# Layer norms with the variance by token on partitions, and one modulation sum moved into the routing

## The chip, the cores and the metric

One core of one Trainium2 chip. The metric is the device time of one launch in microseconds (us): the median of several runs. All five engines of the core are used: TensorE (PE), VectorE (DVE), ScalarE (ACT), GpSimd (POOL) and SyncE (SP), which issues the DMAs.

## What is computed

One inference step of a trunk of four layers on 384 tokens (128 of context, 256 latent) with a width of 1024. The mixer of layer i is gMLP, SSD, HGRN2 and gMLP again; behind each stands a mixture of 16 experts. Each half of a layer ends in a layer norm, so there are eight:

```python
def layer_norm(x, g, b):
    mu = jnp.mean(xf, -1, keepdims=True)
    var = jnp.mean(jnp.square(xf - mu), -1, keepdims=True)
    return (xf - mu) * lax.rsqrt(var + LN_EPS) * g + b

sh1, sc1, g1, sh2, sc2, g2 = modulation(cond, w_mod[li], b_mod[li])
h = x * (1 + sc1) + sh1
x = layer_norm(ALPHA * x + g1 * mixer(h), ln_g[li, 0], ln_b[li, 0])
h = x * (1 + sc2) + sh2
x = layer_norm(ALPHA * x + g2 * moe(h), ln_g[li, 1], ln_b[li, 1])
```

`modulation` is silu(cond) @ w_mod + b_mod, 1024 x 6144 for each layer. The SSD mixer has an RMS norm of its own ahead of its output matrix.

## The kernel before

Activations lie with features on partitions: `x`, `y` and `h32` are 8 tiles (KD) of 128 features by 384 tokens (T), and NT = 3 blocks of 128 tokens. Every engine runs its own hand-written order; semaphores order them, and `claim(bank, ...)` makes TensorE wait until a PSUM bank's last reader is through. Dense products of the mixers split both operands in a high and a low part (ACT makes `whi`, POOL `wlo`) and take three products.

The norm of `q` (0 to 7; two for each layer, 2l behind the mixer and 2l+1 behind the experts): `mean_step` adds each residual tile as it comes, with a 128x128 matrix of 1/D as weights, so that bank 6 holds the mean of each token on all partitions. DVE subtracts it in four pieces (L1765), ACT squares them (L1275), `variance(q)` multiplies the same matrix with the 8 square tiles into bank 5 (L1508, 384 columns), ACT takes the root of 128x384 (L1277), DVE the reciprocal of 128x384 (L1768), and then eight times multiplies a tile (L1770) and modulates it (L1755). ACT and, behind the experts, POOL make `x`, `hh` and `hl` of each tile. In layer 1 `squares(j)` (L718) does the same for the RMS norm, beside the SSD's last steps, and root and reciprocal follow (L575, L853); the result scales each out tile (L857).

The out stage (`out_tiles`) makes 8 tiles with `full`; DVE adds each to the residual, and the mean step of a tile follows one tile later. Modulation is worked out beside it: w_mod comes in chunks of 1 MB, 24 for each layer in 6 groups of 4. DVE multiplies a chunk into `macc` (`mod_chunk`, L1722 and L1725, four operations), and when a group is through TensorE sums over partitions (`mod_sum`, L1492: 16 products, which the trace shows as 32 instructions, with `macc` as weights and one column of ones) and DVE takes the result (`mod_take`, L1733). `out_mods` says which chunks lie ahead of which out tile, for SP's loads and for DVE, and `sums_after` after which tile the sum stands: after tile 3 and tile 7 in layers 0 and 1, after tile 7 in layers 2 and 3. The sum after tile 7 of layers 0 to 2 is the next layer's first group (6l+6); that of layer 3 is its own last group.

All loads go through SP's one queue in the order of `stream_plan`. In the mixers they rotate through four narrow slots of 1 MB (RAW = 4): a load waits until the chunk four places earlier is used up, an out chunk by TensorE, a mod chunk by DVE. The experts use eight slots.

Behind norm 2l stands the routing: router products of 16 columns (L1586), transposes (L1577), group ranks (L1597, L1599), then DVE works out slots and the `spread` matrices (L1881), and TensorE gathers the tokens (L1609, L1610) ahead of the experts (L1646, L1661).

## Time and profile before

| | us |
|---|---|
| median of 3 runs | 3042.9 (3038.44 to 3047.69) |
| the profiled execution | 3040.79, of which its span is 3039.0 |
| TensorE busy | 2660.4 (88%) |
| DVE busy | 1495.8 (49%) |
| POOL busy | 800.3 (26%) |
| ACT busy | 745.4 (25%) |
| mean granted clock of TensorE | 0.916 |

The profile is of one execution. Line numbers are those of the kernel before. A timeline row gives the start and the length of one or more instructions of a line in us, and in brackets how long the engine was idle ahead and what ended that. TensorE's instructions are pipelined, so a row's length holds the drain of its last one; the distance from one start to the next is its price in a stream. PEclk is the granted clock, as a share of 2.4 GHz.

### The profile page before, as it was taken

The numbers are of one execution on the slowest core, as the hardware profiler recorded it, in microseconds if no ns is written. First come the engines' busy times: TensorE is split into PE (matmuls) and PEld (weight loads), VectorE is DVE, ScalarE is ACT, GpSimd is POOL, SyncE is SP. The second block draws the span as 40 slices with busy tenths as digits, with TensorE's granted clock in tenths as the row PEclk, the third lists the DMA queues.
The fourth block names the chain that finished last, engine by engine and source line by source line (L and its number), as shares of the span: only waits on it lengthen the run. The fifth ranks groups of instructions, "written<-read, shape, count | busy, mean of one in ns | idle before, by whom it ended". The sixth has DMA issues, their size and how long they took to land.

```text
span 3039.0 us, 30686 instructions
## 1 busy us (share of the span) xinstructions
PE 2660.4 (88%) x11926; PEld 1949.3 (64%) x11926; DVE 1495.8 (49%) x2416; ACT 745.4 (25%) x1253; POOL 800.3 (26%) x501
## 2 busy tenths in 40 slices
PE   1679889998897888899998877778999989989997
PEld 1679864445896778744457866667444589974444
DVE  7445543333649876533334478875333326650012
ACT  0123130001453342310014243333100144231001
POOL 1346400001453344000014457650000146600000
PEclk9889879999799999799998887788999999979999
DMA  6543638893231215388943410113889433437881
GB/s 222 166 125 98 185 108 326 320 363 125 87 120 33 66 59 163 115 299 323 352 173 117 139 59 18 33 58 124 299 323 351 174 111 111 125 125 256 298 302 50
DMA packets 291855, 524.44 MB, mean 173 GB/s; under 512 B 9472, under 2 KB 141056, under 8 KB 291328
## 3 DMA queue, kind: packets, MB, share of 16 engines
q1 hardware_dynamic: 288256, 519.33, 49.3%
q10 hardware_dynamic: 3456, 3.15, 0.3%
q8 instruction: 96, 1.57, 0.2%
q14 instruction: 47, 0.39, 0.0%
HBM read 517.73 MB, written 4.72 MB: 172 GB/s over the span
## 4 chain that ended last, share of the span: by engine, by line
PE 74%; DVE 14%; issue 4%; ACT 4%; DMA 3%; POOL 2%; ACTq 0%; SPq 0%; DVEq 0%
PE ps L1646 22%; PE ps L1661 11%; PE ps L1458 6%; PE ps L1459 6%; PE ps L1460 6%; PE ps L1492 3%; DVE macc L1725 3%; PE ps L1508 2%; PE ps L1481 2%; PE ps L1482 2%; PE ps L1483 2%; POOL wlo L1391 1%; DVE h L1755 1%; PE ps L654 1%; PE ps L1500 1%
## 5 line engine op out<-in xcount | busy, mean ns | idle before, releaser
L1391 POOL TENSOR_TENSOR wlo<-ring,whi 128x1024 fp32r<-128x1024 f32 x202 | 525.5, 2616 | 1515.2 <-ACT whi L1263 1515.2
L1646 PE MATMUL ps<-ring,xg 128*128 128x512 f32 x1536 | 705.3, 604 | 0.0
L1646 PEld LDWEIGHTS ps<-ring,xg 128*128 128x128 f32 x1536 | 289.5, 194 | 327.9 <-issue 327.5
L1725 DVE SCALAR_TENSOR_TENSOR macc<-ring,cond_s,macc 128x1024 f32<-128x1024 f32 x336 | 452.8, 1409 | 0.0
L1936 DVE SCALAR_TENSOR_TENSOR hid<-ps,cws,sg 128x256 f32<-128x256 f32 x96 | 46.4, 483 | 671.4 <-ACT sg L1356 671.4
L1661 PE MATMUL ps<-ring,hidt 128*128 128x512 f32 x768 | 351.7, 601 | 2.3 <-ACT hidt L1330 2.3
L1458 PE MATMUL ps<-hh,whi 128*128 128x384 f32 x832 | 306.2, 368 | 28.3 <-POOL wlo L1391 18.4
L1263 ACT ACTIVATE whi<-ring 128x1024 fp32r<-128x1024 f32 x202 | 206.9, 1054 | 352.7 <-DMA ring<-gmlp_w_out 115.8
L1459 PE MATMUL ps<-hl,whi 128*128 128x384 f32 x832 | 291.0, 350 | 0.0
L1460 PE MATMUL ps<-hh,wlo 128*128 128x384 f32 x832 | 290.8, 350 | 0.0
L1661 PEld LDWEIGHTS ps<-ring,hidt 128*128 128x128 f32 x768 | 147.9, 193 | 188.7 <-issue 188.7
L1330 ACT ACTIVATE hidt<-ps 128x256 f32<-128x256 f32 x96 | 36.9, 384 | 750.8 <-PE ps L1636 750.8
L1481 PE MATMUL ps<-whi,hh 128*128 128x256 f32 x480 | 144.8, 302 | 67.3 <-POOL wlo L1391 58.8
L1458 PEld LDWEIGHTS ps<-hh,whi 128*128 128x128 f32 x832 | 167.0, 201 | 37.6 <-POOL wlo L1391 20.0
L1459 PEld LDWEIGHTS ps<-hl,whi 128*128 128x128 f32 x832 | 166.9, 201 | 0.7 <-issue 0.5
L1460 PEld LDWEIGHTS ps<-hh,wlo 128*128 128x128 f32 x832 | 165.9, 199 | 0.0
L1481 PEld LDWEIGHTS ps<-whi,hh 128*128 128x128 f32 x480 | 99.6, 207 | 69.8 <-POOL wlo L1391 59.7
L1482 PE MATMUL ps<-whi,hl 128*128 128x256 f32 x480 | 142.9, 298 | 0.0
L1483 PE MATMUL ps<-wlo,hh 128*128 128x256 f32 x480 | 142.5, 297 | 0.0
L1492 PE MATMUL ps<-ones,macc 128*128 128x1 f32 x768 | 100.2, 264 | 46.2 <-DVE macc L1725 46.2
L1492 PEld LDWEIGHTS ps<-ones,macc 128*128 128x128 f32 x768 | 101.8, 215 | 52.3 <-issue 31.5
L1458 PE MATMUL ps<-gsh,whi 128*128 128x384 f32 x256 | 91.0, 355 | 19.8 <-POOL wlo L1391 19.2
(325 smaller groups left out, 4175.3 us busy)
## 6 DMA issues: line engine op xcount, KB each, us to landing
ring<-moe_w_gu SPq DMA_DIRECT2D x192, 1024.0 KB, 7.5
ring<-w_mod SPq DMA_DIRECT2D x96, 1024.0 KB, 7.6
ring<-moe_w_down SPq DMA_DIRECT2D x96, 1024.0 KB, 5.3
ring<-gmlp_w_in SPq DMA_DIRECT2D x32, 1024.0 KB, 5.7
ring<-ssd_w_in SPq DMA_DIRECT2D x21, 1024.0 KB, 5.3
ring<-hgrn_w_in SPq DMA_DIRECT2D x20, 1024.0 KB, 5.2
ring<-gmlp_w_out SPq DMA_DIRECT2D x16, 1024.0 KB, 5.8
ring<-ssd_w_out SPq DMA_DIRECT2D x8, 1024.0 KB, 5.9
```

Source lines behind the costliest of these rows:

```text
L1263: act.activation(split_sub(whi, s0), raw_sub(s0), ACT.Copy).then_inc(S["hi_ready"], 1)
L1391: pool.tensor_tensor(split_sub(wlo, s0), raw_sub(s0), split_sub(whi, s0).bitcast(F32), ALU.subtract).then_inc(S["lo_ready"], 1)
L1458: pe.matmul(out, lhi, rhi, start=first, stop=False)
L1459: pe.matmul(out, lhi, rlo, start=False, stop=False)
L1460: return pe.matmul(out, llo, rhi, start=False, stop=last)
L1481: pe.matmul(outs[t], hh[:, k, tk], pair(whi, k), start=(k == 0), stop=False)
L1482: pe.matmul(outs[t], hl[:, k, tk], pair(whi, k), start=False, stop=False)
L1483: ins = pe.matmul(outs[t], hh[:, k, tk], pair(wlo, k), start=False, stop=(k == KD - 1))
L1492: ins = pe.matmul(ps[:, 7, 2 * j + v:2 * j + v + 1], macc[:, v, j * P:(j + 1) * P], ones[:, 0:1], start=True, stop=True)
L1646: ins = pe.matmul(ps[:, s % 2, :], xg[:, w, k, :], whole(what, s, 4)[:, k % 4, :], start=(k == 0), stop=(k == KD - 1))
L1661: ins = pe.matmul(ps[:, OUT_BANKS[w % 2][h], :], hidt[:, s % 2, k, :], whole("D", s, 2)[:, k, 512 * h:512 * h + 512], start=(e == 0 and k ...
L1725: ins = dve.scalar_tensor_tensor(out=macc[:, v, :], in0=w[:, k, :], scalar=by, in1=macc[:, v, :], op0=ALU.mult, op1=ALU.add)
```

## The change

Variance: the squares become the weights and one column of the 1/D matrix moves, one product for each of 8 tiles and 3 token blocks, so that the variance of a token lies on its partition, in 3 columns of bank 7. Root and reciprocal work on 128x3. TensorE spreads the result: for each block it multiplies the column, broadcast to 128x128, with the identity, which puts it for each token on all partitions of bank 7, where DVE's multiplication reads it. The RMS norm of layer 1 is made the same way, but with a copy by ACT to SBUF; TensorE waits for the reciprocal ahead of its out products, and DVE's reciprocal stands ahead of `start_residual`.

The next layer's first modulation sum (group 6l+6) leaves the end of the out stage; TensorE does it behind the ranks, and DVE takes it behind the route. `out_mods` gives every tile one chunk until there are none, which changes layer 3 alone (tiles 0 to 3 in place of 1, 3, 5, 7), and its sum stands after tile 3.

```diff
--- before.py
+++ after.py
@@ -147,7 +147,8 @@
 
     todo = ([(l, MODC - MOD_GROUP + j) for j in range(MOD_GROUP)] if l % 3 < 2 else []) + \
            ([(l + 1, j) for j in range(MOD_GROUP)] if l + 1 < DEPTH else [])
-    return todo[c * len(todo) // outs:(c + 1) * len(todo) // outs]
+    each = max(1, len(todo) // outs)
+    return todo[c * each:(c + 1) * each]
 
 
 class Chain:
@@ -230,8 +231,8 @@
 
         sq = ar("ln_sq", [P, KD, T], F32, 0)
         h32 = ar("h32", [P, KD, T], F32, 12)
-        std = ar("ln_std", [P, T], F32, 84)
-        rstd = ar("ln_rstd", [P, T], F32, 86)
+        std = ar("ln_std", [P, NT], F32, 84)
+        rstd = ar("ln_rstd", [P, NT], F32, 86)
 
         macc = ar("macc", [P, 2, D], F32, 76)
 
@@ -295,6 +296,7 @@
         sgy = ar("sgy", [P, 2, T], F32, 81)
         ssq = ar("ssq", [P, 2, T], F32, 84)
         srr = ar("srr", [P, T], F32, 87)
+        rms = ar("rms", [P, 2, NT], F32, 88.5)
         sout = ar("sout", [P, 2, T], F32, 0)
         s0 = yr("s0", [P, 2, 512], F32, 0)
         s1 = yr("s1", [P, 2, 512], F32, 4)
...
@@ -572,7 +574,9 @@
                     act.activation(syh[:, j - 1, :], sgy[:, (j - 1) % 2, :], ACT.Copy).then_inc(S["syh_ready"], 1)
             feed(sb((l, "out")) + 3)
             act.wait_ge(S["rms_done"], 16)
-            act.activation(srr[:, :], bank(6), ACT.Sqrt, bias=eps[:, 0:1], scale=0.5).then_inc(S["rms_std"], 1)
+            act.activation(rms[:, 0, :], ps[:, 6, T:T + NT], ACT.Sqrt, bias=eps[:, 0:1], scale=0.5).then_inc(S["rms_std"], 1)
+            act.wait_ge(S["rms_spread"], 1)
+            act.activation(srr[:, :], bank(6), ACT.Copy).then_inc(S["srr_ready"], 1)
             for m in range(8):
                 feed(sb((l, "out"), 2 * m + 2) + 3)
 
@@ -715,10 +719,12 @@
 
             def squares(j):
                 pe.wait_ge(S["gsq_ready"], j + 1)
-                pe.matmul(bank(6), mean_d[:, :], ssq[:, j % 2, :], start=(j == 0),
-                          stop=(j == 15)).then_inc(S["rms_done"], 1)
-
-            claim(6, "rms_std", 1)
+                for t in range(NT):
+                    ins = pe.matmul(ps[:, 6, T + t:T + t + 1], ssq[:, j % 2, toks(t)], mean_d[:, 0:1], start=(j + t == 0),
+                                    stop=(j == 15 and t == NT - 1))
+                ins.then_inc(S["rms_done"], 1)
+
+            claim(6, "srr_ready", 1)
             for j in range(16):
                 if j % 2 == 0 and j < 8:
                     f = SCAN_Z + j // 2
@@ -730,6 +736,10 @@
                     squares(j - 2)
             squares(14)
             squares(15)
+            pe.wait_ge(S["rms_rec"], 1)
+            for t in range(NT):
+                ins = pe.matmul(ps[:, 6, toks(t)], rms[:, 1, t:t + 1].to_broadcast([P, P]), ident[:, :], start=True, stop=True)
+            ins.then_inc(S["rms_spread"], 1)
             out_tiles(l, syh, syl, 2, "syl_ready", 0)
 
         def dve_ssd(dve, l, link, start_residual, residual, out_chunk_mods, mod_take):
@@ -847,10 +857,11 @@
                 if j >= 2:
                     dve.wait_ge(S["syl_ready"], j - 1)
                 dve.tensor_scalar(sgy[:, j % 2, :], xs[:, j, :], c_("sng", j), None, ALU.mult).then_inc(S["gy_ready"], 1)
+            dve.wait_ge(S["rms_std"], 1)
+            dve.reciprocal(rms[:, 1, :], rms[:, 0, :]).then_inc(S["rms_rec"], 1)
             start_residual(2 * l)
             dve.wait_ge(S["syl_ready"], 16)
-            dve.wait_ge(S["rms_std"], 1)
-            link(dve.reciprocal(srr[:, :], srr[:, :]))
+            dve.wait_ge(S["srr_ready"], 1)
             for m in range(KD):
                 out_chunk_mods(l, m, 1)
                 dve.wait_ge(S["sub_done"], nth[sb((l, "out"), 2 * m + 1)] + 1)
@@ -1245,11 +1256,7 @@
 
         def sums_after(l, m):
 
-            if l % 3 == 2:
-                done = {7: 6 * l + 6}
-            else:
-                done = {3: 6 * l + 5, 7: 6 * l + 6} if l + 1 < DEPTH else {7: 6 * l + 5}
-            return [done[m]] if m in done else []
+            return [6 * l + 5] if l % 3 < 2 and m == 3 else []
 
         @block.scalar
         def _(act):
@@ -1274,7 +1281,7 @@
                     act.wait_ge(S["diff_ready"], 4 * q + j + 1)
                     act.activation(sq[:, 2 * j:2 * j + 2, :], y[:, 2 * j:2 * j + 2, :], ACT.Square).then_inc(S["sq_ready"], 1)
                 act.wait_ge(S["var_done"], q + 1)
-                act.activation(std[:, :], bank(5), ACT.Sqrt, bias=eps[:, 0:1]).then_inc(S["std_ready"], 1)
+                act.activation(std[:, :], ps[:, 7, T:T + NT], ACT.Sqrt, bias=eps[:, 0:1]).then_inc(S["std_ready"], 1)
                 l, w = q // 2, q % 2
                 for k in range(KD):
                     act.wait_ge(S["norm_ready"], 8 * q + k + 1)
@@ -1502,11 +1509,17 @@
                     ins.then_inc(S["mean_done"], 1)
 
             def variance(q):
-                claim(5, "std_ready", q + 1)
+                claim(7, "norm_ready", 8 * q + 8)
                 for k in range(KD):
                     pe.wait_ge(S["sq_ready"], 4 * q + k // 2 + 1)
-                    ins = pe.matmul(bank(5), mean_d[:, :], sq[:, k, :], start=(k == 0), stop=(k == KD - 1))
+                    for t in range(NT):
+                        ins = pe.matmul(ps[:, 7, T + t:T + t + 1], sq[:, k, toks(t)], mean_d[:, 0:1], start=(k + t == 0),
+                                        stop=(k == KD - 1 and t == NT - 1))
                 ins.then_inc(S["var_done"], 1)
+                pe.wait_ge(S["rstd_ready"], q + 1)
+                for t in range(NT):
+                    ins = pe.matmul(ps[:, 7, toks(t)], rstd[:, t:t + 1].to_broadcast([P, P]), ident[:, :], start=True, stop=True)
+                ins.then_inc(S["rstd_spread"], 1)
 
             def out_tiles(l, rhi, rlo, halves, ready, count):
 
@@ -1598,6 +1611,8 @@
                 for u in range(NT):
                     ins = pe.matmul(ps[:, 4, 12:16], ones_b[:, :], gone[:, u, :], start=(u == 0), stop=(u == NT - 1))
                 ins.then_inc(S["rank_done"], 1)
+                if l + 1 < DEPTH:
+                    mod_sum(6 * l + 6)
 
                 pe.wait_ge(S["tlo_ready"], 2 * NT * (l + 1))
                 pe.wait_ge(S["spread_ready"], NT * (l + 1))
@@ -1765,9 +1780,10 @@
                     dve.tensor_tensor(y[:, 2 * j:2 * j + 2, :], y[:, 2 * j:2 * j + 2, :],
                                       bank(6).unsqueeze(1).to_broadcast([P, 2, T]), ALU.subtract).then_inc(S["diff_ready"], 1)
                 dve.wait_ge(S["std_ready"], q + 1)
-                link(dve.reciprocal(rstd[:, :], std[:, :]))
+                dve.reciprocal(rstd[:, :], std[:, :]).then_inc(S["rstd_ready"], 1)
+                dve.wait_ge(S["rstd_spread"], q + 1)
                 for k in range(KD):
-                    dve.tensor_tensor(y[:, k, :], y[:, k, :], rstd[:, :], ALU.mult).then_inc(S["norm_ready"], 1)
+                    dve.tensor_tensor(y[:, k, :], y[:, k, :], bank(7), ALU.mult).then_inc(S["norm_ready"], 1)
                     if not last:
                         dve.wait_ge(S["norm_ready"], 8 * q + k + 1)
                         modulate(y, k)
@@ -1915,6 +1931,8 @@
                 for i in range(NT):
                     tokens_low(l, i)
                 route(l)
+                if l + 1 < DEPTH:
+                    mod_take(6 * l + 6)
                 dve.wait_ge(S["cws_done"], l + 1)
                 dve.tensor_reduce(cws[:, :, :], ps[:, 5, 0:2 * EG * NW].rearrange("p (w h e) -> p w e h", h=2, e=EG), AX.X,
                                   ALU.add).then_inc(S["cws_ready"], 1)
```

## Rows read from the trace of the kernel before

**Rows 1.** The page's chain of work that ended last, by engine.
```profile
PE 74%; DVE 14%; issue 4%; ACT 4%; DMA 3%; POOL 2%; ACTq 0%; SPq 0%; DVEq 0%
```
**Rows 2.** Timeline, layer 0's first norm: start us, us, engine, line, operation [idle before].
```profile
385.33 3.63 PE L1492 MATMUL ps<-ones,macc 128*128 128x1 f32 x32
388.82 2.25 PE L1500 MATMUL ps<-y_t,mean_d 128*128 128x384 f32 x4
393.15 6.97 PE L1508 MATMUL ps<-ln_sq,mean_d 128*128 128x384 f32 x16 [2.08 <-ACT ln_sq L1275]
...
400.77 2.55 DVE L1768 RECIPROCAL ln_rstd<-ln_std 128x384 f32<-128x384 f32 x1 [6.05 <-ACT ln_std L1277]
403.36 0.56 DVE L1770 TENSOR_TENSOR y_t<-y_t,ln_rstd 128x384 f32<-128x384 f32 x1
```
**Rows 3.** Groups by form, variance products: count | busy us, mean ns | idle before.
```profile
L1508 PE MATMUL ps<-ln_sq,mean_d 128*128 128x384 f32 x128 | 55.2, 596 | 16.6 <-ACT ln_sq L1275 16.6
```
**Rows 4.** Timeline, TensorE, the first modulation sum of the kernel.
```profile
25.78 6.96 PE L1492 MATMUL ps<-ones,macc 128*128 128x1 f32 x32 [25.78 <-DVE macc L1725]
```
**Rows 5.** Timeline, TensorE: sum and first variance product, layers 1, 2 and 3.
```profile
1230.42 4.84 PE L1492 MATMUL ps<-ones,macc 128*128 128x1 f32 x32
...
1240.11 0.98 PE L1508 MATMUL ps<-ln_sq,mean_d 128*128 128x384 f32 x1 [2.08 <-ACT ln_sq L1275]
...
2069.14 3.96 PE L1492 MATMUL ps<-ones,macc 128*128 128x1 f32 x32
...
2077.95 0.98 PE L1508 MATMUL ps<-ln_sq,mean_d 128*128 128x384 f32 x1 [2.08 <-ACT ln_sq L1275]
...
2678.87 3.63 PE L1492 MATMUL ps<-ones,macc 128*128 128x1 f32 x32
...
2686.49 0.98 PE L1508 MATMUL ps<-ln_sq,mean_d 128*128 128x384 f32 x1 [2.08 <-ACT ln_sq L1275]
```
**Rows 6.** Windows: us, busy (count) by engine, then PEclk, DMA share, GB/s.
```profile
1233.00:1240.00 7.00, 5.03 (x15) 3.27 (x15) 2.65 (x8) 0.86 (x2) 0.00 (x0) 0.50 1.00 368
2679.00:2683.00 4.00, 4.00 (x35) 3.83 (x34) 1.17 (x5) 0.00 (x0) 0.77 (x1) 1.00 0.93 356
420.20:423.50 3.30, 0.26 (x10) 0.17 (x7) 2.99 (x13) 0.60 (x1) 0.00 (x0) 1.00 0.00 0
1269.00:1273.00 4.00, 0.00 (x0) 0.00 (x0) 3.66 (x15) 0.32 (x1) 0.00 (x0) 0.50 0.00 0
```
**Rows 7.** Timeline, TensorE, layer 0's second norm: last product, first variance product.
```profile
745.50 0.34 PE L1683 MATMUL ps<-back,olo 128*128 128x384 f32 x1
...
749.67 0.56 PE L1508 MATMUL ps<-ln_sq,mean_d 128*128 128x384 f32 x1 [2.08 <-ACT ln_sq L1275]
```
**Rows 8.** Timeline lines for the small operations, and the SSD residual's group.
```profile
2015.22 0.28 ACT L935 ACTIVATE hrt<-ps,eps 128x24 f32<-128x24 f32 x1
...
430.49 0.18 DVE L1901 RECIPROCAL rt<-rt 128x3 f32<-128x3 f32 x1
...
2000.17 1.65 PE L1070 MATMUL ps<-uw 128*128 128x128 f32 x6
...
L857 DVE TENSOR_TENSOR sout<-ps,srr 128x384 f32<-128x384 f32 x8 | 4.4, 556 | 22.7 <-PE ps L1460 22.7
```
**Rows 9.** Timeline, TensorE, layer 0's routing: the first gather product.
```profile
425.47 0.76 PE L1609 MATMUL ps<-spread,thi 128*128 128x512 f32 x1 [5.01 <-DVE spread L1881]
```
**Rows 10.** Timeline, TensorE, out stages: layer 0's tiles 0 and 2, layer 3's tile 0.
```profile
290.79 0.42 PE L1458 MATMUL ps<-gsh,whi 128*128 128x384 f32 x1
...
322.38 0.66 PE L1458 MATMUL ps<-gsh,whi 128*128 128x384 f32 x1 [11.34 <-POOL wlo L1391]
...
2601.22 0.42 PE L1458 MATMUL ps<-gsh,whi 128*128 128x384 f32 x1
```
**Rows 11.** Timeline, layer 1's out stage: ACT's root, TensorE's tile 2.
```profile
1150.33 0.58 ACT L575 ACTIVATE srr<-ps,eps 128x384 f32<-128x384 f32 x1
...
1170.65 0.66 PE L1458 MATMUL ps<-syh,whi 128*128 128x384 f32 x1 [6.86 <-POOL wlo L1391]
```

## What the change will do to the time

> **What bounds the kernel now.** I read the chain of work that ended last first: TensorE carries 74% of it, DVE 14% [rows 1]. So I walk TensorE's timeline through each stage that the diff touches and ask what it waits for there. Around each of the eight layer norms all work is in one line: mean, differences, squares, variance product, root, reciprocal, first multiplication [rows 2]. A microsecond won or lost there is one of the whole. TensorE's time depends on its granted clock, 1.00 (2.4 GHz) or 0.50 (1.2 GHz), so I read that for each stretch too.
>
> **The norm itself, before.** In layer 0 the variance takes 6.97 us (16 instructions: each fp32 product is two). From its end (400.12) to the first multiplication (403.36) it is 3.24 us, of which the reciprocal is 2.55 [rows 2]. All eight variances together are busy for 55.2 us [rows 3]: 6.9 each. Layer 0's 0.44 us an instruction lies between 0.32 and 0.64, which is 768 columns (384 in two passes) at 2.4 and at 1.2 GHz: 5.1 or 10.2 us for 16.
>
> **Variance after.** 8 x 3 products of one column with the squares as weights, in two passes: 48 instructions. The nearest rows are the modulation sums, 32 instructions of exactly that form (128x128 fp32 weights, one column): 3.49 us from the first to the next line's start at the high clock [rows 2], 6.96 us at the low one [rows 4]. That is 0.109 and 0.218 us each, so 48 take 5.2 or 10.45 us. At either clock this equals the 384-column form: fewer columns win nothing, since the weights' load is the price. What differs is the clock. Sums of one column let it fall: in layer 1 the sum began at 1230.42 at full clock and the clock was 0.50 by 1233.00; in layer 3 it began at 2678.87 and was still at 1.00 at 2683.00 [rows 5, 6]. So it falls between some 2 and a little over 4 us after wide products stop. The new variance starts 2.08 us after the mean's last product [rows 7], under that same kind of work, and wants 5.2 us: in all eight norms the clock falls inside it, after 0 to 3.4 us, and nothing in it brings it back (today's wide variance does). I take 1.7 us at full clock: 2 x 5.2 - 1.7 = 8.8 us (rounded up), 70.4 for eight. Against 55.2 that is **+15.2 us** (all of it low: +28.4; all high: -13.6).
>
> The Trainium skill ("TensorE: Matmul & The Clock Gate", LDWEIGHTS) prices a weight load by its columns alone, 128/1.2 = 107 ns, without the clock. It matches the high-clock row and not the low-clock row (218 ns), so the measurement decides. By the page an estimate for 48 would be 5.1 us always, and the sum would be some 29 us less; its time is in rival A.
>
> **Root, reciprocal and spread after.** The root of 24 columns took 0.28 us, the reciprocal of 3 columns 0.18 [rows 8]; I take 0.25 for 3 columns from the first. The spread is 6 instructions of 128 columns. Six of that form took 1.65 us at the low clock [rows 8], which is where the variance leaves it. With five hand-overs of about 0.04 us: 0.25 + 0.18 + 1.65 + 0.2 = 2.3 us, against 3.24. The eight multiplications read PSUM instead of SBUF: 0.56 us in the SSD residual, which does so today, against 0.56 [rows 2, 8], so I cost that at nothing. **-1.0 us x 8 = -8.0** (with the spread at half that time, -13.6). The new waits (TensorE for the reciprocal, DVE for the spread) hold up only what needs the norm's result anyway: behind them stand the router or the next mixer's products, and the eight multiplications. The norm as such thus loses some 7 us. After the norm the router (16 columns) and the other followers begin at the low clock as now.
>
> **The sum taken off the end of the out stage, layers 0 to 2.** Before, TensorE does the sum (3.5 us) between the last out product and the last two mean steps, and the clock falls on those. From the sum's start to the mean's end (variance start - 2.08): 5.74, 7.61 and 6.73 us in layers 0, 1, 2, and 5.54 in layer 3 [rows 2, 5]. The second norms have no sum there: from the last product (start 745.50, the next would be due at 745.68) to 747.59 it is 1.9 us [rows 7]. Layer 1 has a multiplication more in its residual (0.55). Gains: 3.8 + 5.15 + 4.8 = **-13.8 us**. The four small DVE operations that prepare the scale lie beside the last mean step and stay hidden.
>
> **Where that sum goes.** Behind the ranks TensorE waits 5.01 us for the spread matrices [rows 9]. The sum takes 3.5 us at full clock and hides; at the low clock 7.0, and holds up the gather by 2.1 us, which TensorE carries to the experts. The clock there was 1.00 in layer 0 and 0.50 in layer 1 [rows 6]: it is low more often than not, after the 16-column router. No DMA moves with it; DVE's take of the result is one small operation and stands behind the whole route, long after the sum, and the gather still runs. Two of three low: **+4 us** (0 to 6.3).
>
> **Layer 3's out stage: the part that the change's name doesn't tell.** The new `out_mods` gives layer 3, which has only four modulation chunks, one for each of tiles 0 to 3 instead of 1, 3, 5, 7, and `sums_after` its sum after tile 3. That is layer 0's pattern. The four narrow ring slots then hold mod, out, mod, out when the stage begins; the third out chunk waits for DVE to finish the first mod chunk, and DVE starts it only after the residual's start. Layer 0 shows the price: TensorE idle for 11.34 us before tile 2 [rows 10]. Whole stages, first out product to sum: layer 0 385.33 - 290.79 = 94.5 us, layer 3 before 2678.87 - 2601.22 = 77.65 us [rows 2, 5, 10]. Layer 3 after: 94.5 + 1.9 to the mean's end; before 77.65 + 5.54. **+13.3 us** (its own end gain is in it). If the stall didn't come, layer 3 would still pay the sum at tile 3, +3.3.
>
> **SSD norm (layer 1).** The 96 narrow instructions in place of 32 wide ones lie between waits for ACT and cost nothing (0.65 us a square at the high clock, either way). But TensorE, which now goes straight from the squares to the out products, will wait for the root first; ACT makes that at 1150.33, behind two weight splits and a table load [rows 11]. With root, reciprocal and spread TensorE starts at about 1152.5. Behind its wait stand the out tiles; ACT's copy of the spread stands ahead of its next splits, which wait for a DMA anyway. On DVE the reciprocal now stands ahead of the residual's start; both then lie behind the root, and the first mod chunk, which had waited for the root before, begins within 1 us of where it did. What takes TensorE's delay up is the stall of 6.86 us that ends at 1170.65, at tile 2 [rows 11]: two tiles at 9 to 9.7 us (77.65 us for eight in layer 3, stalls included) from 1152.5 end at 1170.5 to 1172. The out chunk for tile 2 is asked for when tile 0 is through, which may now be some 3 us later than today; some of the stall stays. **+1 us** (-2 to +6).
>
> **Sum.** +15.2 - 8.0 - 13.8 + 4 + 13.3 + 1 = +11.7 us. The profiled run took 3040.8 us, so 3052.5. The median of the runs is 2.1 us above that run; I put the forecast between, at **3053**.
>
> **Rivals.**
> - A, faster: one-column products keep the clock up, or their load doesn't slow with it. For it: the clock falls only some time after the wide products stop [rows 6], and not at a fixed one. Against it: [rows 4, 5, 6], and 2.08 us idle ahead. Then variances cost 41.6 instead of 70.4 and the spread 0.9 instead of 1.65: -28.8 - 5.6, 3018 us (3023 with the load alone). It ends on the other side. 8%.
> - B, within the noise: layer 3's new order finds its data in time, since its DVE is free earlier. For it: layer 3's out tiles needn't all wait for DVE. Against it: the same holds in layer 0, with the same queue, and it stalls [rows 10]. It decides if tile 2 starts within some 3 us of tile 1's end: -10, 3043 us. 17%.
> - C, more than I sum: the routed sum at low clock in all three layers (+2.3), the variances wholly at the low clock (+13.2), the SSD wait not taken up (+5). Parts of these together: 3062 to 3072. 15%.
> - The forecast case, 3045 to 3062: 60%, a little over half of it above 3052.
>
> **How the numbers follow.** What a measurement can tell from no change is about 0.3%, 9 us: 3033.8 and 3052.0 are the bounds. Slower: C and about 35 of the 60, with a little of B's upper end: 0.52. Same: the rest of the forecast case and most of B: 0.39. Faster: A and a tail: 0.09. The range leaves out A and the far end of C: 3037 to 3067. Cases of both signs are weighed, but the forecast's own range is 3045 to 3062.
>
> **What would show it.** In the profile after: one-column variance instructions at 0.109 and then 0.218 us, with the clock at 0.50 by the end of each, about 8.8 us a norm; reciprocals of 0.18 us; spreads near 1.65 us; out stages of layers 0 to 2 ending 1.9 us before the differences; the sum in the routing beside an idle TensorE, with a gather some 2 us later where the clock is low; a stall near 11 us at tile 2 of layer 3. I am wrong if the clock is 1.00 through the variances (A), if that stall is missing (B), or if the experts' stages change length, which no part here touches.

## The result: 0.5% slower

| | before | after |
|---|---|---|
| median, us | 3045.35 (3033.82 to 3049.18) | 3058.56 (3044.3 to 3068.47) |
| profiled span, us | 3039.0 | 3054.5 |
| TensorE busy, us | 2660.4 | 2708.4 |
| DVE busy, us | 1495.8 | 1456.9 |
| mean granted clock | 0.916 | 0.904 |

Each has 17 runs, taken side by side. The ratio is 1.005, with a 95% interval of 1.0038 to 1.0061. The forecast was 3053, the most likely sign was slower. One execution of a later kernel (x9) took 4587.21 us at a mean granted clock of 0.629; it is left out of that kernel's median and ratio.

The page of after, its busy times and its chain by engine:

```profile
PE 2708.4 (89%) x12300; PEld 2028.1 (66%) x12300; DVE 1456.9 (48%) x2416; ACT 742.9 (24%) x1254; POOL 794.8 (26%) x501
...
PE 76%; DVE 12%; ACT 4%; issue 3%; DMA 3%; POOL 2%; ACTq 0%; SPq 0%; DVEq 0%
```

DVE has become 39 us less busy and TensorE 48 us more. The chain has moved the same way, from PE 74% and DVE 14% [rows 1] to 76% and 12%.

Layer 0's first norm in the timeline of after (start us, length us, engine, line, operation, [idle before]):

```profile
387.61 0.91 PE L1507 MATMUL ps<-y_t,mean_d 128*128 128x384 f32 x2 [0.19 <-DVE y_t L1800]
390.60 10.06 PE L1516 MATMUL ps<-mean_d,ln_sq 128*128 128x1 f32 x48 [2.08 <-ACT ln_sq L1282]
...
400.70 0.26 ACT L1284 ACTIVATE ln_std<-ps,eps 128x3 f32<-128x3 f32 x1 [6.36 <-PE ps L1516]
401.00 0.18 DVE L1783 RECIPROCAL ln_rstd<-ln_std 128x3 f32<-128x3 f32 x1 [8.83 <-ACT ln_std L1284]
401.23 1.65 PE L1521 MATMUL ps<-ident,ln_rstd 128*128 128x128 f32 x6 [0.56 <-DVE ln_rstd L1783]
402.91 0.56 DVE L1786 TENSOR_TENSOR y_t<-y_t,ps 128x384 f32<-128x384 f32 x1 [1.74 <-PE ps L1521]
```

Set beside [rows 2]: the variance takes 10.06 us in place of 6.97, and from its end (400.66) to the first multiplication it is 2.25 us in place of 3.24. Of those 2.25, root and reciprocal are 0.44 and the spread 1.65.

The windows of the same stretch of after (busy time and count of PE, PEld, DVE, ACT, POOL, then the granted clock, DMA share, GB/s):

```profile
387.00:390.00 3.00, 1.33 (x4) 0.30 (x2) 2.55 (x8) 0.39 (x1) 0.62 (x1) 1.00 0.88 322
390.00:393.00 3.00, 2.40 (x13) 2.43 (x14) 2.17 (x3) 2.94 (x4) 0.00 (x0) 0.66 0.91 318
393.00:396.00 3.00, 3.00 (x15) 3.00 (x16) 0.00 (x0) 1.33 (x2) 0.00 (x0) 0.50 1.06 412
396.00:401.00 5.00, 4.67 (x22) 4.58 (x22) 0.00 (x0) 0.26 (x1) 0.00 (x0) 0.50 1.02 407
401.00:403.00 2.00, 1.65 (x6) 1.35 (x6) 0.26 (x2) 0.00 (x0) 0.00 (x0) 0.50 1.05 390
```

0.66 as a mean over the second window is 0.96 us at 1.00 and the rest at 0.50. In the third window PEld, the loading of weights, is busy for 3.00 of 3.00 us: the loads fill the stream. The variance starts at 390.60, so if the fall stands at 390.96 it ran for 0.4 us at 2.4 GHz and otherwise at 1.2 GHz, and so does the spread. The groups of after, by form (count | busy us, mean ns | idle before):

```profile
L1516 PE MATMUL ps<-mean_d,ln_sq 128*128 128x1 f32 x384 | 76.4, 335 | 16.6 <-ACT ln_sq L1282 16.6
L1521 PE MATMUL ps<-ident,ln_rstd 128*128 128x128 f32 x48 | 13.2, 448 | 4.5 <-DVE ln_rstd L1783 4.5
```

76.4 us answers to the 55.2 of [rows 3]: the new variances cost 21.2 us more. The spread adds 13.2 us that had no counterpart.

The moved sum in layer 0's routing, layer 3's tile 2, and the SSD norm of layer 1, in the timeline of after:

```profile
419.89 6.97 PE L1499 MATMUL ps<-ones,macc 128*128 128x1 f32 x32
...
2631.26 0.66 PE L1465 MATMUL ps<-gsh,whi 128*128 128x384 f32 x1 [11.34 <-POOL wlo L1398]
...
1150.94 0.26 ACT L577 ACTIVATE rms<-ps,eps 128x3 f32<-128x3 f32 x1
1151.23 0.18 DVE L861 RECIPROCAL rms<-rms 128x3 f32<-128x3 f32 x1 [4.06 <-ACT rms L577]
1151.46 1.65 PE L741 MATMUL ps<-ident,rms 128*128 128x128 f32 x6 [3.35 <-DVE rms L861]
1152.77 0.67 PE L1465 MATMUL ps<-syh,whi 128*128 128x384 f32 x1
...
1171.97 0.41 PE L1465 MATMUL ps<-syh,whi 128*128 128x384 f32 x1 [0.40 <-POOL wlo L1398]
```

The stall of 11.34 us, which layer 0 has [rows 10], now stands in layer 3 as well. In layer 1 the out products start at 1152.77 (before: 1146.05) and the stall at tile 2 has shrunk from 6.86 us [rows 11] to 0.40.

To see where the span's 15.5 us went I cut both timelines at the same events: the first DVE difference of each norm, the first variance product, the first multiplication, the first gather product, the first expert product. Everything not in this table differs by less than 1 us in each stage (the experts, their products back, the second norms' differences).

| us, profiled executions | before | after | moved |
|---|---|---|---|
| variance start to first multiplication, eight norms | 81.1 | 94.4 | +13.3 |
| start of kernel to layer 0's differences | 391.18 | 388.63 | -2.55 |
| layer 1's mixer, to its differences | 479.83 | 474.11 | -5.72 |
| layer 2's mixer | 471.53 | 465.16 | -6.37 |
| layer 3's mixer | 244.19 | 258.64 | +14.45 |
| first multiplication to first gather product, four layers | 86.85 | 90.22 | +3.35 |
| rest | | | -1 |

Each column is one execution, and the mixers of other kernels with the same out stage spread by several us. So I also took the mean of each mixer over all profiled executions: with the sum at the out stage's end (before, x3, x4) layers 0, 1 and 2 take 390.6, 480.5 and 473.2 us, with the sum moved (the other nine) 387.9, 478.2 and 466.6. That is -2.7, -2.4 and -6.7, together 11.7 us and not 14.6. Layer 1 alone runs from 474.1 to 481.5 us in the nine.

### The profile page after: what moved, and what is told of

The parts are those of the page before. It is cut to its first block, busy times and chain, and to the rows that moved or that the text cites. A ratio compares the mean times of both kernels' runs of the same rounds, so it can differ in the third digit from the quotient of the medians.

```text
span 3054.5 us, 31434 instructions
## 1 busy us (share of the span) xinstructions
PE 2708.4 (89%) x12300; PEld 2028.1 (66%) x12300; DVE 1456.9 (48%) x2416; ACT 742.9 (24%) x1254; POOL 794.8 (26%) x501
## 4 chain that ended last, share of the span: by engine, by line
PE 76%; DVE 12%; ACT 4%; issue 3%; DMA 3%; POOL 2%; ACTq 0%; SPq 0%; DVEq 0%
PE ps L1661 22%; PE ps L1676 11%; PE ps L1465 6%; PE ps L1466 6%; PE ps L1467 6%; PE ps L1499 3%; PE ps L1516 3%; DVE macc L1740 2%; PE ps L1488 2%; PE ps L1489 2%; PE ps L1490 2%; PE ps L658 1%; DVE h L1770 1%; POOL wlo L1398 1%; PE ps L1599 1%
## 5 line engine op out<-in xcount | busy, mean ns | idle before, releaser
L1740 DVE SCALAR_TENSOR_TENSOR macc<-ring,cond_s,macc 128x1024 f32<-128x1024 f32 x336 | 432.2, 1348 | 0.0
L1499 PE MATMUL ps<-ones,macc 128*128 128x1 f32 x768 | 107.6, 274 | 46.3 <-DVE macc L1740 46.3
L1488 PEld LDWEIGHTS ps<-whi,hh 128*128 128x128 f32 x480 | 100.8, 210 | 65.3 <-POOL wlo L1398 59.1
L1499 PEld LDWEIGHTS ps<-ones,macc 128*128 128x128 f32 x768 | 108.8, 228 | 52.5 <-issue 31.4
```

The costliest lines, as they stand in the source:

```text
L1488: pe.matmul(outs[t], hh[:, k, tk], pair(whi, k), start=(k == 0), stop=False)
L1499: ins = pe.matmul(ps[:, 7, 2 * j + v:2 * j + v + 1], macc[:, v, j * P:(j + 1) * P], ones[:, 0:1], start=True, stop=True)
L1740: ins = dve.scalar_tensor_tensor(out=macc[:, v, :], in0=w[:, k, :], scalar=by, in1=macc[:, v, :], op0=ALU.mult, op1=ALU.add)
```

## The experiments

The theory: the narrow variance isn't slow by itself, but the clock falls in it; moving the sum wins; layer 3's order costs as much as both cost or win. The rivals: the new form costs by its waits or its weight loads; layer 3's order is harmless. Ratios are against the kernel before in the same job; each experiment's stage numbers come from its one profiled execution.

### Layer 3's order alone put back (x1_l3_old)

```diff
-    each = max(1, len(todo) // outs)
-    return todo[c * each:(c + 1) * each]
+    return todo[c * len(todo) // outs:(c + 1) * len(todo) // outs]
...
-            return [6 * l + 5] if l % 3 < 2 and m == 3 else []
+            return [6 * l + 5] if l % 3 < 2 and m == (3 if l + 1 < DEPTH else 7) else []
```

> The changed kernel with layer 3's modulation chunks ahead of tiles 1, 3, 5, 7 and its sum after tile 7, as before; all else changed. Main theory (the third out chunk waits behind the first modulation chunk, an idle TensorE of 11.3 us ahead of tile 2 of layer 3): the stall is gone, the time falls by 12 to 14 us against the changed kernel, which leaves it within 3 us of the kernel before. Rival (the sum in mid-stage and the clock it costs are what layer 3 pays): only 3 to 5 us fall away, 1.003 to 1.004 of before.

Measured: 3049.26 against 3042.09, 1.0029 (1.0014 to 1.0043), so some 6 us less than after's ratio. Layer 3's mixer in its profile takes 244.75 us, 13.9 less than after and as long as before. The stage says what was forecast; the whole kernel kept some 9 us above before, where I had expected at most 3, and its ratio is the one that the rival gave. The routing took some of it back: its four stretches are 93.5 us in x1, against 90.2 in after.

### Layer 3's chunks shifted by one tile (x7_l3_shift)

```diff
     each = max(1, len(todo) // outs)
-    return todo[c * each:(c + 1) * each]
+    c -= outs == 8 and len(todo) == 4
+    return todo[c * each:(c + 1) * each] if c >= 0 else []
...
-            return [6 * l + 5] if l % 3 < 2 and m == 3 else []
+            return [6 * l + 5] if l % 3 < 2 and m == (3 if l + 1 < DEPTH else 4) else []
```

> The changed kernel with layer 3's chunks ahead of tiles 1 to 4 and its sum after tile 4: the same work and the same mid-stage sum, but the first narrow slots hold out, mod, out, mod, so that the third out chunk waits for TensorE's tile 0 and not for DVE's first modulation chunk. Main theory: the stall ahead of tile 2 shrinks from 11.3 us to 3 or less, the sum in mid-stage still costs 3 us or so: 8 to 10 us less than the changed kernel, about 1.001 to 1.002 of before. Rival (the mid-stage sum is the cost): no change against the changed kernel, 1.005.

Measured: 3045.89, 1.0015 (1.0003 to 1.0027). Layer 3's mixer: 249.12 us. The groups of TensorE in its out stage:

```profile
L1466 PE MATMUL ps<-gsh,whi 128*128 128x384 f32 x128 | 44.9, 351 | 2.3 <-POOL wlo L1399 2.3
...
L1500 PE MATMUL ps<-ones,macc 128*128 128x1 f32 x32 | 7.0, 353 | 2.4 <-DVE macc L1741 2.4
```

The 11.34 us stall is gone (2.3 us of waiting for `wlo` in the whole stage). What stays is the sum in mid stage, at the low clock (7.0 us, as in [rows 4]) and with 2.4 us of waiting for DVE. All profiled executions by order: new order 258.6, 254.6 and 255.6 us (after, x2, x6), old order 244.2, 244.8, 245.9, 246.4, 246.5, 246.6, 247.0 and 244.7 (before, x1, x3, x4, x5, x8, x9, x10). The means are 256.3 and 245.8: the order costs 10.5 us. By x7's one profile, 249.1, the stall is some 7 of them and the mid-stage sum 3.4.

### The moved sum alone (x5_sum_only)

```diff
-            if l % 3 == 2:
-                done = {7: 6 * l + 6}
-            else:
-                done = {3: 6 * l + 5, 7: 6 * l + 6} if l + 1 < DEPTH else {7: 6 * l + 5}
-            return [done[m]] if m in done else []
+            return [6 * l + 5] if l % 3 < 2 and m == (3 if l + 1 < DEPTH else 7) else []
...
                 ins.then_inc(S["rank_done"], 1)
+                if l + 1 < DEPTH:
+                    mod_sum(6 * l + 6)
...
                 route(l)
+                if l + 1 < DEPTH:
+                    mod_take(6 * l + 6)
```

> The kernel before with one edit: the next layer's first sum (layers 0 to 2) is done in the routing; norms and layer 3 as before. Theory: the out stages end 1.9 us before the differences, 13.8 us gained at their ends, 3 to 4 given back where the sum runs at the low clock beside the waiting gather: 10 to 11 us less than before, 0.9965. Rival (the gather or the experts pay for the sum in full): no gain, 1.000.

Measured: 3030.37, 0.9965 (0.9952 to 0.9978). The stages to the differences of layers 0 to 2 lost 3.19, 5.13 and 7.51 us, together 15.8. The profiled run, 3022.78, was the fastest of its seven, so this is at the long end; the medians lie 11.7 us apart. The routing stretches are 22.12, 20.74, 20.70 and 20.85 us: no longer than before's 86.85 together. The sum and the first gather product of layer 0 in its timeline:

```profile
417.18 3.93 PE L1488 MATMUL ps<-ones,macc 128*128 128x1 f32 x32
...
422.33 0.76 PE L1607 MATMUL ps<-spread,thi 128*128 128x512 f32 x1 [1.23 <-issue]
```

The sum is the part of the change that wins.

### The new layer norms alone (x3_norm_only)

On the kernel before, the `variance` of the diff above with root, reciprocal and spread; sums, SSD norm and layer 3 as before.

> The kernel before with the new layer norms alone (one-column variance, 3-column root and reciprocal, spread); the sum stays at the end of the out stages, the RMS norm and layer 3 as before. Theory: variances of 9 to 10.4 us each in place of 6.9, spread 1.65, no long reciprocal: +13 to +16 us, 1.0045 to 1.005. Rival (narrow norms gain in themselves and the sum in the routing is what costs): 0.998 or less.

Measured: 3050.8 against 3042.09, 1.0028 (1.0017 to 1.004): slower, but less than the 1.0045 to 1.005 expected. Its profile has 98.7 us in the eight stretches from variance to multiplication, 17.6 more than before; but the profiled run, 3058.07, was the slowest of its six, 7 above their median, and had the lowest mean granted clock (0.905, the others 0.907 to 0.911). So 17.6 is at the long end of what the norms cost there. Its variance group:

```profile
L1509 PE MATMUL ps<-mean_d,ln_sq 128*128 128x1 f32 x384 | 80.7, 346 | 16.6 <-ACT ln_sq L1275 16.6
```

### The old layer norms in the kernel after (x2_wide_norm)

The same edit the other way: `variance`, root, reciprocal and multiplication of before, all else of after.

> The changed kernel with the layer norms as before (wide variance, root and reciprocal of 384 columns); the sum in the routing, layer 3's new order and the new RMS norm stay. By the one-edit runs so far (sum -0.35%, norm +0.28%) and layer 3's stall (+13 us), this should be 3 to 6 us above before, 1.001 to 1.002, and 8 to 12 below the changed kernel. Rival (the norm costs more beside the moved sum than alone, because before the sum had already let the clock fall): up to 15 us below the changed kernel, 1.000.

Measured: 3037.85 against 3044.59, 0.9976 (0.9966 to 0.9986), against 1.005 for after. The new norms so cost 0.74% here, 22 us, and only 0.28% when they stand alone: both expectations missed, in the direction of the interaction, and further than it was expected. Its variance group:

```profile
L1515 PE MATMUL ps<-ln_sq,mean_d 128*128 128x384 f32 x128 | 46.6, 521 | 16.6 <-ACT ln_sq L1282 16.6
```

46.6 us where before has 55.2. A stretch from wide variance to multiplication takes either some 8.6 us, when the clock stays up, or 10.0 to 11.7 when it falls: before has 81.1 us for eight, x5 79.2, x4 75.8, x2 72.5, a mean of 77.1 with no order in which norms are hit. The four kernels with narrow variances and no added products ahead of them have 94.4 (after), 92.3 (x1), 93.7 (x7) and 98.7 (x3), a mean of 94.8. Between the means lie 17.7 us. So the profiled execution of before, from which I took the 6.9 us of a wide variance, was the dearest of these four.

### The SSD norm alone (x4_rms_only)

```diff
-                pe.matmul(bank(6), mean_d[:, :], ssq[:, j % 2, :], start=(j == 0),
-                          stop=(j == 15)).then_inc(S["rms_done"], 1)
+                for t in range(NT):
+                    ins = pe.matmul(ps[:, 6, T + t:T + t + 1], ssq[:, j % 2, toks(t)], mean_d[:, 0:1], start=(j + t == 0),
+                                    stop=(j == 15 and t == NT - 1))
+                ins.then_inc(S["rms_done"], 1)
```

with the root, reciprocal, spread, ACT's copy and DVE's new order of the diff above.

> The kernel before with the new RMS norm of layer 1 alone. Theory: TensorE waits for the root ahead of its out products and starts some 6 us late, and the stall ahead of tile 2 takes nearly all of that up: -2 to +3 us, 1.000. Rival (the wait is paid in full): +6 us, 1.002.

Measured: 3042.8, 0.9995 (0.9981 to 1.0008). The six and more microseconds that TensorE starts later disappear in the stall at tile 2, as the rows of after above show and x4's own timeline too, with 1.37 us in place of 6.86 [rows 11]:

```profile
1171.47 0.41 PE L1468 MATMUL ps<-syh,whi 128*128 128x384 f32 x1 [1.37 <-POOL wlo L1401]
```

### Wide products ahead of the narrow variance (x6_warm)

While TensorE waits for the first squares it multiplies three times 384 columns of constants, into a bank that nobody reads at that time. Nothing else of after changes.

```diff
                 claim(7, "norm_ready", 8 * q + 8)
+                pe.wait_ge(*release[5])
+                for _ in range(3):
+                    pe.matmul(ps[:, 5, 0:T], mean_d[:, :], cols[:, 0:T], start=True, stop=True)
```

> The changed kernel with three more wide products (384 columns, constants, into a bank that nobody reads) put into TensorE's idle 2.08 us ahead of each narrow variance. Main theory (the clock falls some 2 to 4 us after wide products stop, and that is what the narrow variance pays): variances of 5.2 to 8.7 us in place of 9.55 on the mean, 1.5 to 3 us less each, some 12 to 24 us less in all, 0.997 to 1.001 of before. Rival (a narrow product costs what it costs because of the weights' load whatever the clock did before): variances unchanged, 1.005.

Measured: 3032.72, 0.996 (0.9946 to 0.9974), against after's 1.005: a little more than the most that I had expected (0.997, 24 us). The timeline of layer 0's first norm in x6:

```profile
387.88 2.10 PE L1515 MATMUL ps<-cols,mean_d 128*128 128x384 f32 x6
390.04 6.97 PE L1519 MATMUL ps<-mean_d,ln_sq 128*128 128x1 f32 x48
397.58 1.65 PE L1524 MATMUL ps<-ident,ln_rstd 128*128 128x128 f32 x6 [0.56 <-DVE ln_rstd L1786]
```

and the windows of the same stretch, in the columns of those of after:

```profile
387.00:390.00 3.00, 2.85 (x8) 1.44 (x8) 2.55 (x8) 0.85 (x1) 0.15 (x1) 1.00 0.89 307
390.00:393.00 3.00, 2.96 (x27) 2.96 (x27) 1.70 (x2) 2.94 (x4) 0.00 (x0) 1.00 0.99 359
393.00:396.00 3.00, 3.00 (x19) 3.00 (x20) 0.00 (x0) 0.88 (x1) 0.00 (x0) 0.64 1.06 415
```

The same 48 instructions take 6.97 us in place of 10.06, since the clock now falls at 393.8 and not at 391.0 (0.64 and 0.66 as means of their windows). The 2.08 us of idle time ahead are filled, at no cost. The groups of all eight norms:

```profile
L1515 PE MATMUL ps<-cols,mean_d 128*128 128x384 f32 x48 | 16.8, 486 | 0.0
...
L1519 PE MATMUL ps<-mean_d,ln_sq 128*128 128x1 f32 x384 | 49.6, 265 | 0.4
```

49.6 us in place of 76.4, without one instruction less. From variance to multiplication it is 67.6 us in place of 94.4; the 26.8 between them are about the 27 us by which the two ratios differ. (The two profiled spans differ by 24.6 us, since layer 1's mixer, in which no filler stands, happened to take 481.4 us here and 474.1 in after.) The same instructions at another clock cost another time: the clock, and what runs ahead, not the form's waits, sets what the new variance costs.

### The same ahead of the wide variance, with the moved sum (x8_sum_warm_wide)

On the kernel before: the edit of x5, and

```diff
                 claim(5, "std_ready", q + 1)
+                pe.wait_ge(*release[7])
+                for _ in range(3):
+                    pe.matmul(ps[:, 7, 0:T], mean_d[:, :], cols[:, 0:T], start=True, stop=True)
```

> The kernel before with the sum in the routing and three wide products in TensorE's idle time ahead of the old, wide variance. Main theory: the clock stays high through the variance, 5.4 us in place of 6.9 on the mean: up to 12 us less than with the sum's move alone (0.9965), 0.993 to 0.995. Rival (the clock falls in that stretch anyway, or the filling delays the first variance product): no gain on 0.9965.

Measured: 3024.91, 0.9934 (0.9921 to 0.9946). Its variances:

```profile
L1507 PE MATMUL ps<-ln_sq,mean_d 128*128 128x384 f32 x128 | 43.3, 492 | 0.4
```

43.3 us, and all eight stretches at 8.56 to 8.67 us, 69.2 together. In layer 3, where the old order has the sum at the end of the out stage, the fillers of the first norm themselves ran at the low clock:

```profile
2674.36 3.37 PE L1504 MATMUL ps<-cols,mean_d 128*128 128x384 f32 x6
```

They took 3.37 us in place of 2.10 and put the variance off: it starts 2.89 us after the first difference, in the other seven norms 1.89. The clock was back at 1.00 for it. So a filler can cost time ahead of the stretch that it shortens; here it was 1 us.

### And ahead of the narrow variance, with the moved sum (x9_sum_warm_narrow)

On the kernel before: the edits of x5, x3 and x6.

> The kernel before with the modulation sum moved into the routing, the new narrow layer norms, and three 384-column filler products ahead of each narrow variance; layer 3's order and the SSD norm stay old. It is x8 with the other form of the norm. My theory: a narrow variance whose clock is kept up costs what a wide one with the clock kept up costs. From the runs so far, variance start to first multiplication is 8.44 us a norm in x6 (narrow, fillers) and 8.65 in x8 (wide, fillers), so eight norms give 1.7 us between them: 0.993 to 0.994 of before (x8 gave 0.9934), and 67 to 70 us for the eight stretches. Rival: the new form has a price apart from the clock (the waits of TensorE for the reciprocal and of DVE for the spread, multiplications that read PSUM): then the stretches are again under 70 us but the span is 5 us or more above x8's 3026, ratio 0.996 or more.

Measured: 3021.26 (median of five), 0.9928 (0.9905 to 0.9951); the eight stretches take 67.4 us. The timeline of layer 0's first norm in x9:

```profile
386.81 2.10 PE L1504 MATMUL ps<-cols,mean_d 128*128 128x384 f32 x6
388.97 6.89 PE L1508 MATMUL ps<-mean_d,ln_sq 128*128 128x1 f32 x48
396.43 1.65 PE L1513 MATMUL ps<-ident,ln_rstd 128*128 128x128 f32 x6 [0.56 <-DVE ln_rstd L1775]
```

and its windows:

```profile
389.00:392.00 3.00, 3.00 (x27) 3.00 (x28) 1.63 (x2) 2.95 (x4) 0.00 (x0) 1.00 0.99 348
392.00:395.00 3.00, 3.00 (x20) 3.00 (x19) 0.00 (x0) 0.81 (x1) 0.00 (x0) 0.64 1.06 416
```

The stretches are as expected, and the ratio isn't distinguishable from x8's: with the clock held up, narrow (67.4 us) and wide (69.2) cost nearly the same. The rival, a price of the new waits, falls. Even so the clock goes in the middle of the variance, and the spread runs at the low one (1.65 us); what the narrow form saves behind the variance it gives back inside it.

### More filling, up to the gather (x10_more_filling)

x8, and

```diff
                 ins.then_inc(S["var_done"], 1)
+                for _ in range(6):
+                    pe.matmul(ps[:, 7, 0:T], mean_d[:, :], cols[:, 0:T], start=True, stop=True)
...
                     if k == KD - 1:
                         ins.then_inc(S["router_done"], 1)
+                    elif k != 4:
+                        pe.matmul(ps[:, 7, 0:320], mean_d[:, :], cols[:, 0:320], start=True, stop=True)
```

> x8 (sum moved, three fillers ahead of the old wide variance) with more filler products: six of 384 columns behind each variance, while TensorE waits for the root and reciprocal, and one of 320 columns after each of the router's groups of narrow products. Theory: the router and what follows it start at the low clock because only narrow products have run before them; with the fillers the granted clock there is 1.00 and each router product goes faster, up to 3 us a layer less in the stretch from the first multiplication to the first gather product, about 0.990 of before. Rival: TensorE waits for DVE's multiplications and modulations there and not for its own clock; then the fillers' own time (0.33 us each at full clock) either hides in these waits (ratio 0.993 to 0.994, as x8) or adds up to 1 us a layer (0.995).

Measured: 3022.99, 0.9926 (0.9905 to 0.9946), the same as x8. The routing stretches are 21.20, 26.31, 24.49 and 20.12 us, against 23.63, 22.13, 22.12 and 20.76 in x8: a gain of 2.4 and 0.6 us in layers 0 and 3, a loss of 4.2 and 2.4 in layers 1 and 2. Its timeline, first layer 0, then layer 1:

```profile
402.53 0.79 PE L1591 MATMUL ps<-cols,mean_d 128*128 128x320 f32 x2
403.15 0.74 PE L1587 MATMUL ps<-wrt,h 128*128 128x16 f32 x6
...
415.14 0.18 PE L1600 MATMUL ps<-gone,below 128*128 128x4 bf16 x1 [1.92 <-DVE gone L1864]
...
1244.93 0.94 PE L1591 MATMUL ps<-cols,mean_d 128*128 128x320 f32 x2
1245.67 1.30 PE L1587 MATMUL ps<-wrt,h 128*128 128x16 f32 x6
1246.81 1.42 PE L1591 MATMUL ps<-cols,mean_d 128*128 128x320 f32 x2
```

In layer 0 the clock stayed at 2.4 GHz (1.00 in each window from 400 to 415 us), and then TensorE waited 1.92 us for DVE ahead of the ranks: part of the theory's gain was there, and the next limit took the rest. In layer 1 the clock fell at about 1245 in spite of the fillers, and from there on they cost 1.2 us each instead of 0.6. The theory's 0.990 isn't the measured ratio, though the interval just doesn't reach it. The rival's first branch, 0.993 to 0.994 as in x8, fits the number, but not for its reason: the fillers didn't all hide in waits. They won in two layers and lost in two, and filling a stretch whose clock then falls loses what it won elsewhere. Why the two layers differ I can't say.

## Why the prediction was right, and which terms were off

It gave 3053 (3037 to 3067) with slower as the likeliest; the sum was +11.7 us for the profiled executions, and +15.5 came. By its steps:

- **Variances: the mechanism right, the size off.** Forecast 70.4 us, measured 76.4; +15.2 against +21.2 over [rows 3]. The mis-sized term is the time at full clock ahead of the fall: I took 1.7 us of each variance. With 9.55 us as the mean, 2 x 5.2 - 9.55 leaves 0.9 (0.1 to 2.6 by norm). The 1.7 was the middle of the 0 to 3.4 us that I allowed, and no row stood behind the upper end: the rows had the clock gone some 2 to a little over 4 us after wide products stopped, and 2.08 of these are idle, so they allow 0 to some 2. The low-clock price (0.218 us an instruction) holds: 48 of them are 10.45 us, and layer 1's variance took 10.37. The rule of the Trainium skill ("TensorE: Matmul & The Clock Gate", LDWEIGHTS), a load priced by its columns without the clock, would have given an estimate of 41 us for all eight. The traces don't agree: 76.4 us, and even with the fillers ahead 49.4 (x9) and 49.6 (x6), where a part of most variances is still at the low clock.
- **Root, reciprocal, spread: right.** 2.3 us forecast, 2.25 measured, the spread 1.65 as taken. Multiplications that read PSUM cost nothing: 0.56 us each in the timeline above, as in [rows 2]. So the tail won 7.9 us (forecast 8.0), and the norms together lost 13.3 (forecast 7.2).
- **The sum off the out stages' ends: right.** -13.8 us, with the SSD norm +1; measured -14.6 with it in. x5 has -15.8 without the SSD norm. Over all profiled executions it is -11.7.
- **The sum in the routing: about right.** +4 forecast, +3.35 measured. It is at the low clock in layer 0 (6.97 us from 419.89 on, beside a TensorE that was idle for 5.01 us there before [rows 9]) and in layer 2. In x5 the routing gets no longer. The narrow norm leaves a low clock to what follows: layers 0 to 2 have 68.1, 71.4 and 65.3 us of routing in after, x1 and x7, against 63.6 and 64.6 in x5 and x2. That is 4 us between the two sets, each of few executions.
- **Layer 3's out stage: right.** +13.3 forecast, +14.45 measured, the stall 11.34 us as in layer 0; undone in x1 it gives back 13.9 in that stage. Over several executions the cost is 10.5, so before's 244.19 was at the short end and after's 258.64 at the long one. If only the sum in mid stage had stayed, +3.3 by the prediction; x7 has +3.4. Rival B falls. By the ratios x1 gave 6 to 7 us back; their intervals together allow some 1 to 12, so 10.5 isn't contradicted.
- **SSD norm: right** (x4 is within 0.1% of before), the stall at tile 2 taking up all of it.
- **Rival C** came in part: the clock was lower in the variances than summed, by 6 us of its 13; its SSD wait didn't cost.
- **Rival A** fell as a forecast, and yet the runs with fillers show what it would have been worth: 26.8 us, where I had worked out 28.8 for the variances. (Its spread term, 5.6 us, is 6.0 by its own numbers; the spread stayed at 1.65 us in x6 and x9.)
- **What was luck.** That the sum came within 4 us of the profiled difference owes something to the two executions that I compared. Before's wide norms were the dearest of four (81.1 us, mean 77.1), and its layer 3 the shortest of eight; by the means the norms cost 17.7 us and not 13.3, layer 3's order 10.5 and not 14.45, and the out stages' ends win 11.7 and not 14.6. The signs and the order of size hold; that single terms fit within 1 us doesn't show that they are known to 1 us.

What stays open: in medians the new norms cost 8.6 us on before and 22 on the kernel with the moved sum (x3; after against x2. x1 against x5, 1.0029 over 0.9965, is close to the latter with 19.5 us, the SSD norm included). The stretches of the norms place 17.6 and 21.9. The routing's 4 us may be a part of the gap. The stretches, taken over more executions, don't show it: 98.7 (x3) less 78.5 (mean of before and x4) is 20 us where the sum stands at the out stage's end, and 93.5 (mean of after, x1, x7) less 75.8 (x5, x2) is 17.7 us where it has moved. So the cause of the difference between 8.6 and 22 us isn't shown.

Six kernels are faster than both, with intervals wholly below 1: x2, x5, x6, x8, x9 and x10. The fastest three are x8, x9 and x10, at 0.9926 to 0.9934: the moved sum (0.9965 alone) and three products on constants ahead of each variance. x9 differs from x5 by the narrow norm with fillers: 11.7 us less in the stretches (79.2 and 67.4), and 0.9928 against 0.9965, 11 us, in the ratios.

## What to carry to other kernels

Price a matmul form by its row at either clock, and ask what TensorE does in the microseconds ahead of it and whether it holds the clock: making an operation narrower saved nothing here, where the weight loads fill the stream, and it left most of it at half the clock. Idle TensorE time ahead of a chain on the critical path can be filled with wide products on constants, but only where TensorE waits anyway and where the trace shows that the clock holds. Compare a stage over several executions before a few us of it are given to a cause. Read the whole diff: two lines of chunk order, named in no title, cost about as much as the largest stated part won (10.5 and 11.7 us).

## What the runs showed of the hardware that I had not expected

- Three wide products (2.10 us) in the wait ahead of a variance moved the clock's fall by some 3 us (from 391 to 394 in layer 0, from the windows of after and x6), which made the 48 narrow instructions 3.1 us shorter.
- Wide products don't hold the clock by being there: in x10's layer 1 it fell at about 1245, among groups of 16 and 320 columns, after 4 us of 384-column products; in layer 0 the same sequence ran at 1.00 to its end.
- The same wide variance takes 8.6 us or 10.0 to 11.7 us to the first multiplication, in changing norms from kernel to kernel; over eight norms that alone moved the profiled executions by 8.6 us (72.5 to 81.1).
